# Four instead of three weight units begin with the first token half behind each normed phase

## The reference

```python
hn  = rms_norm(h, pre_g)                    # before the sub-layer
mix = sublayer(hn)                          # gMLP, attention, or conv_ffn
h   = h + rms_norm(mix, post_g)             # after it
f   = conv_ffn(rms_norm(h, pre_ffn_g), w_up, conv_w, conv_b, w_down)
h   = h + rms_norm(f, post_ffn_g)
```

## Time and profile before

| | |
|---|---|
| time, median of 3 runs | 2141.34 us |
| the profiled execution's own time | 2140.77 us |
| its span (first to last instruction) | 2139.0 us |
| PE busy | 2129.6 us, 100% of the span |
| DVE, ACT, POOL busy | 1432.1, 1014.8, 72.7 us |
| granted PE clock | 0.999 of full speed |
| HBM read | 404.10 MB, 190 GB/s over the span |

### The profile page before, as it was taken

One profiled execution on the slowest core, in us unless ns is written; L12 is line 12 of the kernel. 1 busy time (PEld: TensorE's weight loads), 2 busy tenths in 40 slices (PEclk: granted clock), 3 DMA queues, 4 the chain that ended last, 5 costly groups with the idle time before them and its releaser, 6 DMA issues.

```text
span 2139.0 us, 32149 instructions
## 1 busy us (share of the span) xinstructions
PE 2129.6 (100%) x11273; PEld 1826.9 (85%) x11273; DVE 1432.1 (67%) x1758; ACT 1014.8 (47%) x1174; POOL 72.7 (3%) x99
## 2 busy tenths in 40 slices
PE   9999999999999999999999999999999999999998
PEld 8888888888888888888888888888888888888887
DVE  5666577777877774444765675577878778774444
ACT  6445464444444444434644574464444444444433
POOL 0510010000000000000000010010000000000000
PEclk9999999999999999999999999999999999999999
DMA  7865656666666566665566544656666666666664
GB/s 258 231 207 176 198 175 190 187 184 196 188 193 187 177 218 199 193 193 180 187 189 189 177 154 154 204 175 189 189 180 198 189 193 187 180 221 192 193 195 149
DMA packets 210686, 407.31 MB, mean 190 GB/s; under 512 B 13488, under 2 KB 15920, under 8 KB 209968
## 3 DMA queue, kind: packets, MB, share of 16 engines
q1 hardware_dynamic: 207920, 398.51, 60.8%
q0 software_dynamic: 2640, 7.73, 1.1%
q10 hardware_dynamic: 48, 0.02, 0.0%
HBM read 404.10 MB, written 2.10 MB: 190 GB/s over the span
## 4 chain that ended last, share of the span: by engine, by line
PE 99%; issue 0%; ACT 0%; DVE 0%; DVEq 0%; POOLq 0%; POOL 0%; ACTq 0%
PE ps L1440 37%; PE ps L1443 18%; PE ps L1456 13%; PE ps L1454 13%; PE ps L1455 13%; PE ps L1407 1%; PE ps L1410 1%; PE ps L1371 1%; PE ps L1533 1%; PE ps L1374 0%; PE ps L1550 0%; PE ps L1612 0%; PE ps L1680 0%; PE ps L1651 0%; PE ps L1512 0%
## 5 line engine op out<-in xcount | busy, mean ns | idle before, releaser
L887 DVE TENSOR_TENSOR w_lo<-raw,w_hi 128x1024 fp32r<-128x1024 f32 x743 | 905.7, 1225 | 633.6 <-ACT w_hi L539 628.3
L539 ACT CAST w_hi<-raw 128x1024 fp32r<-128x1024 f32 x749 | 781.3, 1050 | 930.3 <-PE ps L1443 526.9
L1440 PE MATMUL ps<-x_parts,w_hi 128*128 128x512 f32 x3136 | 1089.3, 394 | 0.0
L1443 PE MATMUL ps<-x_parts,w_lo 128*128 128x256 f32 x3136 | 869.7, 277 | 0.0
L1440 PEld LDWEIGHTS ps<-x_parts,w_hi 128*128 128x128 f32 x3136 | 588.1, 188 | 137.2
L1443 PEld LDWEIGHTS ps<-x_parts,w_lo 128*128 128x128 f32 x3136 | 589.1, 188 | 0.0
L1454 PE MATMUL ps<-w_hi,g_parts 128*128 128x512 f32 x704 | 274.1, 389 | 0.0
L1456 PE MATMUL ps<-w_hi,g_parts 128*128 128x512 f32 x704 | 273.9, 389 | 0.0
L1455 PE MATMUL ps<-w_lo,g_parts 128*128 128x512 f32 x704 | 273.9, 389 | 0.0
L1455 PEld LDWEIGHTS ps<-w_lo,g_parts 128*128 128x128 f32 x704 | 132.1, 188 | 27.4
L1456 PEld LDWEIGHTS ps<-w_hi,g_parts 128*128 128x128 f32 x704 | 132.1, 188 | 27.4
(11 more groups left out here) (163 smaller groups left out, 1740.8 us busy)
## 6 DMA issues: line engine op xcount, KB each, us to landing
raw<-in_ffn_w_up SPq DMA_DIRECT2D x352, 512.0 KB, 3.7
raw<-in_ffn_w_down SPq DMA_DIRECT2D x176, 512.0 KB, 4.5
raw<-in_a_w_in SPq DMA_DIRECT2D x61, 512.0 KB, 4.6
raw<-in_a_w_out SPq DMA_DIRECT2D x32, 512.0 KB, 4.7
raw<-in_b_w_q SPq DMA_DIRECT2D x32, 512.0 KB, 4.5
raw<-in_w_k SPq DMA_DIRECT2D x32, 512.0 KB, 4.6
raw<-in_w_v SPq DMA_DIRECT2D x32, 512.0 KB, 4.7
raw<-in_b_w_o SPq DMA_DIRECT2D x32, 512.0 KB, 4.6
```

Source lines behind the costliest of these rows:

```text
L539: act.copy(w_hi[:, slot, :, :], raw[:, slot, :, :]).then_inc(unit_hi, 1)
L887: dve.tensor_tensor(w_lo[:, slot, :, :], raw[:, slot, :, :], w_hi[:, slot, :, :].bitcast(F32), ALU.subtract).then_inc(unit_split, 1)
L1440: pe.matmul(ps[:, bank + m, :], w_hi[:, slot, kk, m * P:(m + 1) * P], src[:, kt, :, :].rearrange("p a t -> p (a t)"), start=first, stop=False,
L1443: mm = pe.matmul(ps[:, bank + m, 0:T], w_lo[:, slot, kk, m * P:(m + 1) * P], src[:, kt, HI, :], start=False, stop=last, skip_group_check=True)
```

## The change

EARLY is 4, so slots 0 to 3 are half 0 of units 0 to 3, slots 4 to 7 half 1, and slots 8 to 11 whole, for units 4 to 7. There are 12 slots instead of 11, with as many transposes in all (32).

- PE begins with half 0 of four units, and turns slot 3 behind unit 0, slots 4 and 5 ahead of unit 3. The last two slots, which are units 6 and 7, are turned behind unit 4 (before: behind unit 3).
- Unit 2 is cast by DVE (`third_high`), no longer by ACT. ACT casts unit 3 ahead of slot 3 (for t = 2, behind slot 3).
- POOL subtracts unit 1 alone, behind the first chunk of half 1 of h. Unit 2's subtraction is DVE's.
- DVE scales the last block of half 1 (`gain_block`) ahead of `update_first`, and its list of slots, units and updates is written anew.
- ACT keeps slots 0 to 7, DVE slots 8 to 11 (t = 2).

```diff
-        EARLY = 3
+        EARLY = 4
         SPLIT_TILES = UK * EARLY
-        SLOT_BANK = [4, 5, 6, 4, 5, 6, 7, 4, 5, 6, 7]
-        SLOT_BEFORE = {3: 0, 4: 1, 5: 2, 7: 3, 8: 4, 9: 5, 10: 6}
+        SLOT_BANK = [4, 5, 6, 4, 5, 6, 7, 4, 5, 6, 7, 4]
+        SLOT_BEFORE = {3: 0, 4: 1, 5: 2, 7: 3, 8: 4, 9: 5, 10: 6, 11: 7}
...
@@ POOL
-                    if s + 1 < len(NORMED):
-                        if half:
-                            pool.wait_ge(h_new[1], NB * s + 2)
-                        unit_low(BEHIND[s], half + 1)
                 if s + 1 < len(NORMED):
+                    pool.wait_ge(h_new[1], NB * s + 1)
+                    unit_low(BEHIND[s], 1)
                     pre_rsqrt(s + 1)
@@ ACT, turn_and_split
-                slot_keep(t, (1,))
-                units(ph.first, 2, 3)
-                slot_high(t, (3, 4))
...
+                act.wait_ge(unit_hi, ph.first + 3)
+                if t != KV_NORM:
+                    units(ph.first, 3, RING)
+                act.wait_ge(evacuated, ph.block0)
+                slot_high(t, (3,))
+                if t == KV_NORM:
+                    units(ph.first, 3, RING)
+                slot_high(t, (4, 5))
+                slot_keep(t, (3, 4))
+                slot_high(t, (6, 7))
+                slot_keep(t, (5,))
                 units(ph.first, RING, RING + 1)
-                slot_keep(t, (5,))
-                slot_high(t, (7, 8))
+                slot_keep(t, (6,))
+                slot_high(t, (8, 9))
+                slot_keep(t, (7,))
+                square_stream(t, 0)
                 units(ph.first, RING + 1, RING + 2)
-                square_stream(t, 0)
-                slot_high(t, (9, 10))
+                slot_high(t, (10, 11))
                 units(ph.first, RING + 2, RING + 3)
...
@@ ACT, after_normed
-                slot_keep(s + 1, (0,))
+                slot_keep(s + 1, (0, 1, 2))
@@ DVE
+            def third_high(ph):
+                dve.wait_ge(raw_loaded[2], 16 * (ph.first // RING + 1))
+                dve.wait_ge(unit_used, ph.first + 2 - RING + 1)
+                dve.wait_ge(unit_hi, ph.first + 2)
+                dve.tensor_copy(w_hi[:, 2, :, :], raw[:, 2, :, :]).then_inc(unit_hi, 1)
...
             def turn_and_split(t, ph):
+                gain_block(t - 1, LAST, (1,))
                 update_first(t - 1)
+                slot_low(t, (3, 4))
                 update_stream(t - 1, 1, 1)
-                slot_low(t, (3,))
-                gain_block(t - 1, LAST, (1,))
-                slot_low(t, (4,))
+                slot_low(t, (5,))
+                dve.wait_ge(unit_split, ph.first + 2)
+                units(ph.first, 2, 3)
                 update_stream(t - 1, 2, 0)
                 update_stream(t - 1, 2, 1)
-                slot_low(t, (5, 6))
-                slot_keep(t, (6,))
-                dve.wait_ge(unit_split, ph.first + EARLY)
+                slot_low(t, (6, 7))
                 units(ph.first, 3, RING)
+                slot_low(t, (8, 9))
+                units(ph.first, RING, RING + 1)
                 update_stream(t - 1, 3, 0)
                 update_stream(t - 1, 3, 1)
...
+                slot_keep(t, (8, 9))
+                units(ph.first, RING + 1, RING + 3)
+                slot_low(t, (10, 11))
                 units(ph.first, RING + 3, ph.units)
...
                 update_stream(s, 1, 0)
+                third_high(nxt)
                 slot_low(s + 1, (0, 1, 2))
@@ PE, first_columns
                 for u in range(EARLY):
+                    if u == 1:
+                        turn_slots(t, (3,))
                     if u == EARLY - 1:
-                        turn_slots(t, (3, 4))
+                        turn_slots(t, (4, 5))
...
                     if u == 0:
-                        turn_slots(t, (5,))
                         pe.wait_ge(evacuated, ph.block0)
-                        turn_slots(t, (6,))
+                        turn_slots(t, (6, 7))
                     if u == 1:
-                        turn_slots(t, (7, 8))
+                        turn_slots(t, (8, 9))
...
                     if u == EARLY:
-                        turn_slots(t, (9, 10))
+                        turn_slots(t, (10, 11))
```

More of the change, by code:

```diff
@@ L617, in turn_and_split @@
             def turn_and_split(t, ph):
-                slot_keep(t, (1,))
-                units(ph.first, 2, 3)
-                slot_high(t, (3, 4))
-                slot_keep(t, (2,))
-                units(ph.first, 3, RING)
-                slot_keep(t, (3,))
-                slot_high(t, (5, 6))
-                slot_keep(t, (4,))
+                act.wait_ge(unit_hi, ph.first + 3)
[9 more added lines that the diff above has]
+                slot_keep(t, (5,))
                 units(ph.first, RING, RING + 1)
-                slot_keep(t, (5,))
-                slot_high(t, (7, 8))
+                slot_keep(t, (6,))
+                slot_high(t, (8, 9))
+                slot_keep(t, (7,))
+                square_stream(t, 0)
                 units(ph.first, RING + 1, RING + 2)
-                square_stream(t, 0)
-                slot_high(t, (9, 10))
+                slot_high(t, (10, 11))
                 units(ph.first, RING + 2, RING + 3)
@@ L968, in turn_and_split @@
             def turn_and_split(t, ph):
+                gain_block(t - 1, LAST, (1,))
                 update_first(t - 1)
+                slot_low(t, (3, 4))
                 update_stream(t - 1, 1, 1)
-                slot_low(t, (3,))
-                gain_block(t - 1, LAST, (1,))
-                slot_low(t, (4,))
+                slot_low(t, (5,))
+                dve.wait_ge(unit_split, ph.first + 2)
+                units(ph.first, 2, 3)
                 update_stream(t - 1, 2, 0)
                 update_stream(t - 1, 2, 1)
-                slot_low(t, (5, 6))
-                slot_keep(t, (6,))
-                dve.wait_ge(unit_split, ph.first + EARLY)
+                slot_low(t, (6, 7))
                 units(ph.first, 3, RING)
+                slot_low(t, (8, 9))
+                units(ph.first, RING, RING + 1)
                 update_stream(t - 1, 3, 0)
                 update_stream(t - 1, 3, 1)
-                slot_low(t, (7,))
-                units(ph.first, RING, RING + 1)
-                slot_low(t, (8,))
-                slot_keep(t, (7, 8))
-                units(ph.first, RING + 1, RING + 2)
-                slot_low(t, (9,))
-                units(ph.first, RING + 2, RING + 3)
-                slot_low(t, (10,))
+                slot_keep(t, (8, 9))
+                units(ph.first, RING + 1, RING + 3)
+                slot_low(t, (10, 11))
                 units(ph.first, RING + 3, ph.units)
-                slot_keep(t, (9, 10))
+                slot_keep(t, (10, 11))
                 pre_means(t)
```

## The result

| | before | after |
|---|---|---|
| median | 2141.06 us (2140.4 to 2141.44, 13 runs) | 2152.76 us (2143.64 to 2162.06, 13 runs) |
| ratio to before | | 1.005 [1.0038, 1.0061] |
| the profiled execution | 2140.77 us | 2143.73 us |
| granted PE clock there | 0.999 | 0.999 |

The change makes the kernel slower by 11.7 us, against a forecast of 3.8. The two rows of the table tell two different things. The execution that was profiled is one of the fastest of after, and it is 2.96 us above that of before. Over the 13 runs the times of after don't lie in one place: 2143.64, 2143.73, 2144.8; 2147.59; seven from 2152.56 to 2154.1; 2156.31; 2162.06. Those of before lie within 1.04 us. So the result has two parts: some 3 us that every execution pays, and 0 to 18 us, most often 9, that come on top from one execution to the next.

What follows compares the result with a forecast made beforehand. PE's queue plus its few waits was taken as the bound. The terms gave +1.14 us for two transitions and +1.49 for the second, +3.8 in all: 2145.1 us from a median of 2141.34, with an 8-in-10 range of 2143.0 to 2147.0.

Steps and rivals of the forecast that it cites:

- 1, the wait of L958 goes: First transposes of half 1 no longer wait for DVE's update of h at L958: -0.77 us a transition.
- 2, one more group: On PE, unit 3 as 24 products (+0.05) and one more transpose group (0.08): +0.13 us a transition.
- 3, DVE's cast: DVE casts unit 2 in 0.75 us, ending before PE wants slot 0's low part: costs 0.
- 4, slot 4: PE waits for slot 4's first two tiles, 0.16 and 0.07 us: +0.23 us a transition.
- 5, unit 4: DVE's row of work up to unit 4 ends late, so PE waits there: +0.2 us, bounds 0 to 0.6.
- 6, unit 6: PE waits behind unit 5 for unit 6 and its slot, the largest term: +1.35 us, bounds 1.1 and 1.6.
- 7, the copy (t = 2): In the second transition PE waits behind unit 0 for ACT to copy slot 0's bank: +0.35 us.
- the time is what PE's queue holds, plus the few places where PE waits: Whole kernel: PE is busy for 100% of the span, and other engines count only where PE waits for them.
- Rivals B to D: DVE's row later, 2146.6 us, 20%; first wait stays, 2146.6, 5%; loads late in a transition, 2148, 4%.

Runs made afterwards that it cites:

- before_wait6: The kernel before, with a DVE wait that holds back unit 6's subtraction until ACT's square of chunk 2, three times; 2148.67 us, 1.0044.
- before_late8: The kernel before, with DVE subtracting unit 8 of the two up phases only after ACT has cast unit 10; 2149.94 us, 1.0042.
- cast6_spread8: cast6_sq_early with eight transposes in the spread instead of two; 2163.0 us, 1.0103.
- cast6_sq_early: cast6_first with ACT's squares of chunks 1 and 2 of h moved ahead of the high parts of slots 10 and 11; 2140.98 us, 1.0012.
- before_kick_gate_u: The kernel before, with two transposes of unused result ahead of the phase gate_u; 2141.12 us, 0.9999.
- before_busy9: The kernel before, with unit 8 still early but DVE subtracting units 9 and 10 across PE's entry into the phase; 2140.89 us, 1.0000.
- after_sq_early: The changed kernel with ACT's squares of chunks 1 and 2 of h moved ahead of slots 10 and 11; 2156.66 us, 1.0083.
- cast6_first: The changed kernel with ACT casting unit 6 ahead of the high parts of slots 10 and 11 instead of behind them; 2148.75 us, 1.0035.
- sq_early_spread3: cast6_sq_early with three transposes in the spread instead of two; 2140.28 us, 1.0007.
- the two kick runs: The kernel before with unused transposes ahead of gate_u: two in one run (2141.12 us, 0.9999), eight in the other (2140.73 us, 0.9999).

## Why the prediction was wrong

**Most terms of the sum held.** In the first transition:

| step | forecast us | measured us |
|---|---|---|
| 1, the wait of L958 goes | -0.77 | gone from the list, no gap at 285.05 |
| 2, one more group | +0.13 | not read apart |
| 3, DVE's cast | 0.75 long, costs 0 | 0.69 long, no wait behind it |
| 4, slot 4 | +0.23 | +0.25 |
| 5, unit 4 | +0.2 | 0 |
| 6, unit 6 | +1.35 | +1.29, and +0.07 inside |
| 7, the copy (t = 2) | +0.35 | +0.29 |
| transitions, first product to spread | +1.14, +1.49, +1.14 | +0.96, +1.36, +1.00 |
| sum | +3.8 | +3.3 in the transitions, +2.96 between the two profiled executions |

Part 6 was the step that decided, and it came from one reading: the row of ACT and DVE in the earlier trace rows needs 4.93 us from the turn to PE's next use, and the change leaves 3.65 us of work on PE beside it. The measured distance is 4.94. Statement for statement, what was said to show it is there: three waits of 1.1 us in the list (1.29 from start to start) on x_parts.

Part 5 was mis-sized. The update of 286.65 took 1.01 us and ended 287.66 - 287.11 = 0.55 behind POOL, as forecast; the steps behind it took some 0.3 us less in all than I gave them. From PE's first product to the end of unit 4's subtraction are 294.30 + 1.21 - 281.97 = 13.54 us; I had 13.87. It is there just in time, and the 0.2 us, three times, are most of what the sum had too much. The Trainium skill (SBUF — State Buffer, "two separate sides") says that DVE, with two SBUF inputs as here, and a GpSimd instruction that reads SBUF share a pair of ports, which the one that starts first holds for its whole instruction while the other is fully blocked. The trace agrees in part: DVE's update is stretched from 0.7 to 1.01 us and ends behind POOL, but only 0.55 us behind it, less than the 0.7 that it takes alone. (By the forecast's own numbers the stretch was 288.05 - 287.14 - 0.7 = 0.2 us, not the 0.3 that it gave; measured it is 0.3.)

**The step that failed** is the first, "the time is what PE's queue holds, plus the few places where PE waits". I took what the queue holds as a constant, and added and removed only around it. It isn't one: with not an instruction changed, a phase costs 346.7 or 353.3 ns a pair, and what PE does in the transition ahead goes with which. With the forecast's mechanism alone the time is 2143.7, inside the range of 2143.0 to 2147.0; the median is 2152.8. In both profiles near that median the first up phase, 168 units long, goes in the slow rhythm, and the times of most executions fit this. None of the rivals had it. Rivals B to D would have made the time longer by waits, and no such wait is there.

Could the profile of before have told? It had the number: 229 products in 40 us in gate_u (110 to 150) against 233 at 1100 to 1140, products of the same shapes, at the same clock and with no wait. That two phases of the same form differ by 2% for nothing that the profile shows was a reason to ask what makes a phase slow, and to widen the range upward by 3 to 9 us for a change that rewrites three entries.

**What is shown, and what is open.** Shown: the 9 us are one up phase at 353.3 ns a pair instead of 346.7, with no wait in it and the granted clock at 1.00 in both. Shown too: a wait of 1.4 us ahead of unit 6 alone can start the slow rhythm (before_wait6; q_in and k_in in the profile); a late unit 8 alone can (before_late8, 4 of 4, in one of the two phases it was late for); idle transposes at the entry alone can turn it on (cast6_spread8 beside cast6_sq_early) and off (before_kick_gate_u, 3 of 10). DVE's subtractions across the entry alone don't (before_busy9).

Made likely, not shown: that in after it is the wait that does it. With unit 8 early the slow phases stay (after_sq_early), and in the profiles units 6 and 7 are slow behind this wait, 14 times in 15, and never without it. But before_wait6 didn't bring after's slow up phase in most executions, and taking the wait away didn't bring before's steadiness back. A late unit 8 isn't the reason for that, since 5 of 12 are still over with it early. In the slow profiles of both kernels (cast6_first, cast6_sq_early) units 6 and 7 come to the third spread in the even rhythm, and in the fast transitions of the same profiles in the fast one.

Open: what in PE's stream holds a rhythm; what sets the rhythm of units 6 and 7 and the place in it, which differ from execution to execution of one kernel; and what in the new order of the transition leaves sq_early_spread3 with 3 of 12.

## What to carry to other kernels

When a change moves a wait to another place, the row of the engine that feeds it is read from its first start to its last and set against what the bottleneck now has beside it; that gave 4.93 us here against 4.94 measured. And the time of a long untouched phase is compared too, by counting instructions in a fixed stretch: 2266 instead of 2309 in 400 us was worth three times what the waits cost. Before one trusts a median of a kernel that is bound by PE, look whether its times form groups, and profile one of each.

## What was not expected of the hardware

- A stream of fp32r products of 512 and 256 columns, each with its weight load, has two lasting costs at a granted clock of 1.00: 384 matmuls in 66.56 us or in 67.84 (346.7 and 353.3 ns a pair). One phase keeps one of them for up to 475 us (466.1 us for the first up phase in after, 475.1 in the profile at 2152.74).
- Which one goes with what the engine did in the microseconds ahead: the rhythm of the products there, the place in it, and the number of transposes behind them. Eight transposes turned a fast stream slow in 4 entries of 4 and a slow one fast in 2 of 2.
- gate_u is slow in every profile but those of the two kick runs, 228 or 229 products in 40 us; two idle transposes ahead of it made it fast in 3 of 10 executions, 2 us less.
